# Two-layer hybrid trunk: order of the last value block and the context, named PSUM banks between the layers, and the place of the keys' squares

## The reference

```python
def latent_layer(x, mod, ctx, lp, alpha):
    ...
    parts, gate = modulate_project(x, mod, w_in)
    qa, ka, va, za, qm, km, vm, om, gm, zm, qw, kw, vw, zw, g_merge = parts
    qa = apply_rope(rms_norm(q_heads(qa, ATT_KV, ATT_GROUP), qk_gain[0]), cos, sin)
    ka = apply_rope(rms_norm(kv_heads(ka, ATT_KV), qk_gain[1]), cos, sin)
    ya = merge_heads(attend_blocks(qa, k_all, v_all, None))
    yw = merge_heads(attend_band(qw, kw, vw, ck_w.astype(kw.dtype), cv_w.astype(vw.dtype), sink))
    ym, _, _, _ = mlstm_bidir(qm, km, vm, om, gm, gate_bias, C0, n0, m0)
    return merge_residual(x, (ya, ym, yw), (za, zm, zw), g_merge, gate, w_branch, w_out, ln_g, ln_b, alpha)
```

## Time and profile before

| | us |
|---|---|
| median of 3 runs | 1621.02 |
| lowest, highest | 1620.31, 1625.83 |
| profiled execution, its own time | 1620.05 |
| its span | 1618.3 |

### The profile page before, as it was taken

How to read it: one execution, slowest core, us unless ns; L and a number is a source line. 1 busy time by engine, 2 the same in 40 slices (tenths; PEclk the granted TensorE clock), 3 DMA queues, 4 the chain that set the end, 5 groups by cost and what they waited for, 6 DMA issues and landing times.

```text
span 1618.3 us, 22438 instructions
## 1 busy us (share of the span) xinstructions
PE 1530.3 (95%) x9011; PEld 1251.8 (77%) x9011; DVE 740.9 (46%) x1442; ACT 471.0 (29%) x1095; POOL 630.6 (39%) x504
## 2 busy tenths in 40 slices
PE   3799999999999999999999899999989999999997
PEld 2689778896688887788878877889757888877886
DVE  3277830357612252622497676116580236252256
ACT  0125730136510122410134376102571003232010
POOL 2173025630145443146672410555103554423562
PEclk9899999999999999999999999999999999999999
DMA  9221002216422222115340100223301222211421
GB/s 340 56 84 50 1 27 79 78 53 215 129 62 77 70 66 66 33 54 181 108 143 27 56 27 1 66 79 92 116 19 40 78 79 65 66 46 40 169 79 65
DMA packets 75992, 128.71 MB, mean 80 GB/s; under 512 B 16173, under 2 KB 20721, under 8 KB 75889
## 3 DMA queue, kind: packets, MB, share of 16 engines
q1 hardware_dynamic: 72416, 118.88, 23.8%
q10 hardware_dynamic: 3472, 8.39, 1.4%
HBM read 120.96 MB, written 6.30 MB: 79 GB/s over the span
## 4 chain that ended last, share of the span: by engine, by line
PE 79%; DVE 10%; issue 3%; ACT 3%; POOL 3%; DMA 1%; ACTq 1%; SPq 0%; POOLq 0%; DVEq 0%
PE pb L966 54%; PE pb L1094 6%; PE pb L1223 3%; PE pb L991 3%; PE pb L1174 2%; PE pb L1137 2%; PE pb L922 1%; PE pb L1145 1%; PE pb L1267 1%; ACTq L1484 1%; PE pb L1404 1%; DMA raw<-in_w_mod 1%; DVE ks L2030 1%; DVE nm L2172 1%; DVE xh L2536 1%
## 5 line engine op out<-in xcount | busy, mean ns | idle before, releaser
L966 PE MATMUL pb<-wsp,act_T 128*128 128x512 f32 x3060 | 719.6, 394 | 15.8 <-DVE act_T L1970 11.8
L966 PEld LDWEIGHTS pb<-wsp,act_T 128*128 128x128 f32 x3060 | 576.6, 190 | 140.7 <-issue 22.0
L820 POOL CAST wsp<-raw 128x1024 fp32r<-128x1024 f32 x128 | 136.5, 1066 | 849.2 <-PE pb L966 680.3
L823 POOL TENSOR_TENSOR wsp<-raw,wsp 128x512 fp32r<-128x512 f32 x268 | 358.9, 1360 | 10.2
L966 PE MATMUL pb<-wsp,yT 128*128 128x512 f32 x720 | 165.7, 390 | 0.0
L966 PEld LDWEIGHTS pb<-wsp,yT 128*128 128x128 f32 x720 | 135.1, 188 | 27.8
L2488 DVE SCALAR_TENSOR_TENSOR mt<-tg,pb 128x512 f32<-128x512 f32 x40 | 27.4, 685 | 230.6 <-PE pb L966 229.7
L1828 ACT ACTIVATE tg<-pb 128x512 f32<-128x512 f32 x60 | 35.9, 599 | 289.6 <-PE pb L966 289.6
L1678 ACT ACTIVATE pr<-pb,nm 128x640 f32<-128x640 f32 (+2 forms) x128 | 91.3, 713 | 4.8 <-DVE nm L2172 4.8
L1174 PE MATMUL pb<-ident,pr 128*128 128x128 f32 x480 | 74.5, 276 | 6.2 <-ACT pT L1713 5.8
L2202 DVE TENSOR_SCALAR pr<-pr,rden 128x640 f32<-128x640 f32 (+2 forms) x128 | 69.8, 545 | 4.5
(11 more groups left out here) (278 smaller groups left out, 1946.5 us busy)
## 6 DMA issues: line engine op xcount, KB each, us to landing
raw<-in_w_in SPq DMA_DIRECT2D x112, 512.0 KB, 3.6
raw<-in_w_mod SPq DMA_DIRECT2D x32, 512.0 KB, 4.7
raw<-in_w_branch SPq DMA_DIRECT2D x24, 512.0 KB, 3.6
raw<-in_w_out SPq DMA_DIRECT2D x16, 512.0 KB, 3.6
stage<-in_w_mod ACTq DMA_DIRECT2D x8, 512.0 KB, 16.1
stage<-in_w_mod SPq DMA_DIRECT2D x8, 512.0 KB, 12.0
raw<-in_w_in SPq DMA_DIRECT2D x16, 256.0 KB, 5.1
xh<-in_x_sample SPq DMA_DIRECT2D x7, 512.0 KB, 7.3
```

Of the source, the lines that this page charges most:

```text
L820: pool.tensor_copy(hi, raw[:, p % 3, :, 0:width]).then_inc(raw_hi, 1)
L823: ins = pool.tensor_tensor(lo[:, j, :], raw[:, p % 3, j, 0:width], hi[:, j, :].bitcast(F32), ALU.subtract)
L966: mm = pe.matmul(dst, lhs(a, k, t), w[:, wa, j, 0:width], start=(k == 0 and n == 0), stop=(i == count - 1 and j == 1 and n == 2))
```

## The change

There are three parts.

1. In both attention branches VectorE's `normalise_context` moves from step `NL + PT_AFTER + 2` to the step after the last `gate_out`, so block 3 is gated first.
2. The banks of the passage are named. For tile t, `kv` has bank 6 or 2 and `q` bank 7 or 3 in turn, and the `xT` pairs keep 4-5 and 0-1. Before, `roll` gave `q` 2, 6, 2, 6, 0 and `kv` 6, 3, 7, 3, 7. The former users change with them: q tile 0 follows layer 0's `("out", 1, 2)` instead of `("out", 1, 3)`, kv tile 1 follows `("out", 1, 3)` instead of `("out", 1, 4)`, and z chunk 0 (banks 0-1) follows only `xT` 3 instead of q tile 4. `rolling = 1` is the value that `roll` had reached, so all later banks stay.
3. At the passage's end VectorE does `k_squares` before `q_path("A", 3)` and `k_path` before `q_lo(3)`; ScalarE does `of_q("A", 4)` and the rounding of z piece 2 before `q_rounded("A", 3)`.

```diff
@@ plan_layer, layer 1 @@
         for t in range(T):
             if t == 0:
-                psum.roll_pair(("xT", 0))
-            psum.roll(("kv", t))
+                psum.take(("xT", 0), 4, 5)
+            psum.take(("kv", t), 6 - 4 * (t % 2))
             if t + 1 < T:
-                psum.roll_pair(("xT", t + 1))
-            psum.roll(("A", "q", t))
+                psum.take(("xT", t + 1), *((0, 1) if t % 2 == 0 else (4, 5)))
+            psum.take(("A", "q", t), 7 - 4 * (t % 2))
+        psum.rolling = 1
@@ ScalarE, attention, (l, br) == (1, "A") @@
-                        hi_part(2)
                         hi_part(3)
                         k_rounded()
@@ ScalarE, end of layer 0 @@
                     of_kv(4)
+                    of_q("A", 4)
+                    hi_piece(pieces.first[1, ("A", "z")] + 2)
                     q_rounded("A", 3)
-                    of_q("A", 4)
@@ VectorE, attention, (l, br) == (1, "A") @@
                         dve.wait_ge(pre_done[l], 4)
-                        k_squares()
+                        k_path(br)
                         q_lo(br, 3)
-                        k_path(br)
                         dve.wait_ge(k_done[l], 1)
@@ VectorE, steps of the sweep @@
-                        if s == NL + PT_AFTER + 2:
+                        if s == NL + PV_AFTER[br] + 1:
                             normalise_context()
@@ VectorE, end of layer 0 @@
                     q_squares(3)
+                    k_squares()
                     q_path("A", 3)
```

## The result

The changed kernel takes **1615.01 us** in the median of nine runs (1613.58 to 1619.72); the kernel before, run in turn with it, takes 1624.35 in the median of nine (1620.31 to 1626.34). The ratio is 0.9949, interval 0.9935 to 0.9962: 8.3 us faster, between 6.2 and 10.6. The forecast was 1610.3 with a gain of 10.7. The plain medians differ by 9.3 us, the means (1623.9 and 1615.6) by 8.3. The sign was right. The time is 4.7 us above the forecast, outside the forecast's own range (1608.5 to 1612.5) and inside the one that has the rivals in it (to 1616); the gain came out 2.4 us smaller. The profiled execution of the changed kernel took 1613.68 us, with a span of 1611.9; that of before had 1618.3. So the two spans differ by only 6.4 us.

The account below looks back on a forecast made before the run. TensorE, 95% busy, was taken as the bound, so gains come from closing its holes or restoring clock: 5.4 (C's end) + 1.4 (q tile 0) + 3.9 (gate path) = 10.7 us, giving 1610.3; range 1607.5 to 1616.

Parts of the forecast that it names:

- C's hole: TensorE's idle time after C's sweep in layer 1, before G: 3.56 us, with 2.7 us of lost clock behind it.
- q tile 0: Passage: named banks let this tile start early, in pieces as weights arrive; kv tile 1 starts 1.4 us earlier.
- Part 1's hole: C's end, layer 1: gating before normalisation shrinks TensorE's idle time from 3.56 to 0.88 us, a gain of 2.7.
- Part 1's clock: G in layer 1: behind the shorter idle time TensorE keeps full clock, thirty matmuls gaining 2.7 us.
- Gate path: Passage's end: the 4.96 us wait goes, about 1.5 us remains at step 8; gain 3.9 us, bounds 2.2 to 5.4.
- what I had called wrong: Signs of failure: clock under 1.00 behind G's start, over 3 us wait before step 8, `rmsk` over 5 us behind q tile 4.
- 0.3 of cover: Passage's end: `rmsk` ends 0.3 us after `q_path(3)`, so longer squares would not delay the keys' chain until then.
- The rule against the step: Passage's end: VectorE and GpSimd exclude each other, squares wait up to 1.45 us, gate-path gain 2.8 instead of 3.9.
- The base: Whole kernel: gains subtracted from the profiled 1620.05 us, then 1.0 us added because the median shown lay that much higher.
- The clock did not fall at what is left of the holes: Rival, 17%: TensorE's clock falls again at the remaining waits; 1613.0 us at C's end, 1614.5 at two places.
- stay down in the passage: Rival, 4%: TensorE stays at 1.2 GHz after an early, piecewise start at 838; slower, 1638.4 us if until 894.
- the keys' path: Rival, 12%: at the gate path VectorE and GpSimd slow each other; chain 2.5 us later, gain 8.2, 1612.8 us.

Follow-up runs that it names:

- the filled hole: Kernel before with 12 matmuls that nobody reads put into TensorE's 3.56 us of idle time at C's end in layer 1; 1622.95 us, ratio 0.9988.
- before's fourth: The kernel before, with no edit, in its fourth profiled execution; 1623.73 us.

## Why the prediction was off: the mechanism held, two sizes and the base did not

The holes went as forecast. What failed is that one execution was read as the rule for TensorE's clock, and this went into three terms: the clock behind C's hole (2.7 us taken, 1.9 shown), q tile 0 (1.4 taken, 0.6 shown) and the time from which the gain was taken (1621.02, shown as 1624.35).

**Part 1's hole: right.** 0.88 forecast, 0.89 measured in every kernel with the swap, released by `ytmp`. The normalisation cost nothing, as said.

**Part 1's clock: a term that failed.** The sum took "the whole 2.7 us" from the one difference 9.83 - 7.09. The clock did stay up behind 0.89, as I chose, but before, it does not fall fully each time: the hole of 3.56 cost 2.8, 0, 1.6, 2.7, 2.7 and 1.6 us of clock. Its mean, and the filled hole by itself, give 1.9. So part 1 is worth 2.7 + 1.9 = 4.6, and was measured at 3.7 (2.3 to 5.0), where the forecast's 5.4 is outside. I had written down beside this term that it would scatter, and left the term as it was.

**q tile 0: right in mechanism, under half the size.** In the first profile kv tile 1 came 1.16 us earlier, close to the 1.4; the waits were 0.94, 1.30 and 0.68 for 0.7, 1.5 and 0.9. But with banks in turn, nine executions give kv tile 1 at 11.19 to 11.29 us in five and at 9.92 to 9.95 in four, by whether the clock falls behind the 3 us hole, mean 10.66. With named banks five give 9.97 to 10.21. So the gain is 1.2 with a fall and nothing without, 0.6 in the mean. That at present a low clock is being paid for here already is true of five of the nine executions, mine among them, and not of the other four. The hole itself brought nothing: it was cut into three waits for weights and for VectorE.

**Gate path: right.** 3.9 forecast, 3.85 in the first profile, 4.2 by the means (69.85 and 65.6). The mean is above the first profile because where the clock doesn't fall at q tile 0, it costs more later: 70.31 to 70.36 in those three of the seven executions of the old order (the first 48 matmuls of the gate path take 9.60 in before's fourth, 8.80 in its first). The waits came out at 0.78, 0.39 and 0.91 for 0.6, 0.5 and 1.5. Step 8 began 18.6 us behind the last q tile, forecast 18.5; the wait before it was shorter because TensorE itself needed 17.7 us up to there and not 16.4 to 16.9. `rmsk` ended 5.0 us behind the last q tile (897.9), forecast 4.7; that is at the edge of what I had called wrong. The squares took 2.2 and not 1.8 (893.65 to 895.86), and `k_path` still found `rmsk` not ready, with 1.22 of wait for 0.3 of cover. The cover came from `q_path(3)`, which took 5.95 us (895.86 to 901.81) and not 7.05, because its first multiply took 0.68 for 1.77. That was luck: I had not foreseen it. I was wrong on whose it is: I had put the hole down to the banks and the order together; the order of ScalarE and VectorE does it alone.

**The rule against the step.** GpSimd's split began at 894.63, inside the squares. The two long instructions kept their length (0.83, 0.82 for 0.82 before), and the small one took 0.58, 0.4 longer than the 0.17 of the same instruction in the profile before. The Trainium skill (SBUF — State Buffer, "Who interferes with whom") would have allowed 1.45 us by the working of the prediction; 0.4 was paid, and it lay in the cover. But it was paid by an instruction with one input, and the rule is about two. The next multiply by `rms`, with two inputs, at 895.86 in the midst of the split, took 0.68, where the same instruction took 1.77 before. Both repeat: the multiply takes 1.77 in all nine executions with the old order of VectorE, where it begins within 0.1 us behind the split, and 0.68 in the five with the new one. So the new order saves 1.1 us of VectorE's time there and pays 0.4; why the multiply is spared isn't settled.

**The base.** I put the result 1.0 us above the profile, by three runs. The medians of before in all later sets are 1624.0 to 1625.0, and the profiled 1620.05 was a cheap execution by 4 to 5 us, with 8.5 us of lost clock in layer 0 where others had up to 11.9. Of the 4.7 us by which the time was missed, 3.3 are this (1624.35 less 1621.02), the largest part; the other 1.4 are the gain, 9.3 by the medians and not 10.7.

**The sum again, with means:** 2.7 + 1.9 + 0.6 + 4.2 = 9.4 us, inside the intervals of the change's two measurements (6.2 to 10.6 and 5.7 to 9.6) but above both middles, 8.3 and 7.6. The parts measured by themselves give 3.7 + 0 + 3.6 = 7.3, so nothing hints at one part helping or spoiling another. The 1 to 2 us between the stages and the ratios stay open; the rest behind G varies by 2.0 us between executions (393.0 to 395.0), by no part that I could name.

**The rivals.** The clock did not fall at what is left of the holes in either profile of the changed kernel, nor stay down in the passage; the keys' path was not the bound beyond the 0.91. The effect that took the gain was none of these: the low clock behind C's hole and at q tile 0 is not paid in every execution, and the one that I read had both. The prediction gave 0.68 to a gain of over half a percent; it came out at 0.51%, with an interval of 0.38 to 0.65% that leaves this open.

**Two slips in the working** change nothing: step 0 by its own terms is 1.78 us and not 1.76, and a gain of 12.2 against the median makes 1608.8 and not 1608.5.

## What to carry to other kernels

Price a hole and the clock behind it as two terms: the holes here repeat to 0.1 us or better, the clock is a draw, and its mean needs several profiled executions or an experiment that fills the hole. Take the time to which a forecast is added from many runs, and not from the three beside the profile. Where a product waits for a bank, look for who reads out the bank next in turn, and move that reader ahead of whatever waits for another engine; and when a copy is moved forward, move what feeds the engine behind it too, or the hole comes back two steps later under another name.

## What the runs showed of the hardware

- A hole of 3.56 us in TensorE's line, the same in every execution, was followed by full clock once and by 1.6 to 2.8 us of lost clock five times; one of about 3 us before q tile 0 by a fall in five of nine. In before's layer 0 one of 2.04 us had a fall behind it in the first execution (426 to 430, 0.59) and none in the second (424 to 436 at 1.00). Behind the holes of 0.62 to 1.26 at C's end there was none in eight.
- Layer 0 of the unchanged kernel took 836.6 to 842.4 us in four executions, with 8.5 to 11.9 us of lost clock, a spread larger than what each single part of this change gives. Lost clock is not always lost time: the fall of 0.59 at 426 us (1.6 us of lost clock) delayed TensorE by 0.5 us, since the wait behind it shrank from 1.14 to 0.28.
- A VectorE multiply of 128x512 took 1.77 us where it began within 0.1 us behind the start of a GpSimd split (nine executions), and 0.68, no longer than alone, where it began 1.2 us into it (five). In these five a small instruction (128x10) shortly after the split's start took 0.57 to 0.59 for 0.17.
